# One block of a projection's products moved into the last softmax steps of the phase before it

## The reference

```python
proj = u @ w_in
qkv_a, z_a, b_a, a_a, q_b, k_b, v_b, gate_a, gate_b = jnp.split(proj, cuts, axis=-1)
qkv_a = silu(causal_depthwise_conv(qkv_a, conv_w))     # 3072 columns, for the delta rule
o_a = gated_delta_rule(q_a, k_a, v_a, g, beta)
y_b = window_attention(q_b, k_b, v_b, sinks, rel_bias) # softmax in bands of three chunks of 64
merged = sigmoid(gate_a) * y_a + sigmoid(gate_b) * y_b
```

## Time and profile before

| | us |
|---|---|
| median of 3 runs (1893.04 to 1895.02) | 1893.08 |
| the profiled execution | 1898.35 |
| its span, from first to last instruction | 1896.4 |
| TensorE busy in the span | 1743.6 |
| VectorE busy | 1428.1 |
| ScalarE busy | 1054.7 |

### The profile page before, as it was taken

One profiled execution on the slowest core, in us unless ns is written; L12 is line 12 of the kernel. 1 busy time (PEld: TensorE's weight loads), 2 busy tenths in 40 slices (PEclk: granted clock), 3 DMA queues, 4 the chain that ended last, 5 costly groups with the idle time before them and its releaser, 6 DMA issues. The chain is left out here.

```text
span 1896.4 us, 35111 instructions
## 1 busy us (share of the span) xinstructions
PE 1743.6 (92%) x14040; PEld 970.1 (51%) x14040; DVE 1428.1 (75%) x1786; ACT 1054.7 (56%) x1335; POOL 383.1 (20%) x262
## 2 busy tenths in 40 slices
PE   4999979999969999989999998499999999999965
PEld 1656654444448888734444455344554444444422
DVE  5556665878877889556766687799998888888928
ACT  3456653355444445342334211498898888888824
POOL 0000000110113434200000000234554344444300
PEclk9999999999988999999999998599999999999988
DMA  8500027563546232061223121599999999999935
GB/s 337 108 23 24 1 76 277 192 234 127 184 125 157 60 96 53 2 214 56 81 86 112 44 89 56 211 419 399 412 407 403 399 397 402 391 394 383 363 135 191
DMA packets 160441, 385.08 MB, mean 203 GB/s; under 512 B 24843, under 2 KB 102276, under 8 KB 132398
## 3 DMA queue, kind: packets, MB, share of 16 engines
q1 hardware_dynamic: 145710, 351.58, 51.0%
q0 software_dynamic: 14592, 31.56, 4.3%
HBM read 354.86 MB, written 48.15 MB: 213 GB/s over the span
## 5 line engine op out<-in xcount | busy, mean ns | idle before, releaser
L2298 PE MATMUL ps<-w_gate_up_split,gathered_t 128*128 128x512 f16 x1680 | 376.8, 381 | 7.7 <-ACT gathered_t L2372 3.3
L2464 DVE SCALAR_TENSOR_TENSOR w_gate_up_split<-w_staged,w_gate_up_split 128x2048 f16<-128x2048 f32 x140 | 318.3, 2288 | 55.0 <-ACT w_gate_up_split L2363 53.6
L2363 ACT ACTIVATE w_gate_up_split<-w_staged 128x2048 f16<-128x2048 f32 x140 | 266.5, 1908 | 44.2 <-DMA w_staged<-in_w_up 12.6
L2298 PEld LDWEIGHTS ps<-w_gate_up_split,gathered_t 128*128 128x128 f16 x1680 | 162.4, 98 | 203.5 <-ACT gathered_t L2372 10.4
L219 PE MATMUL ps<-u_transposed,w_gates_split 128*128 128x512 f16 x1152 | 254.3, 383 | 6.2 <-PEq L144 3.1
L825 PE MATMUL ps<-u_transposed,w_dense_split 128*128 128x512 f16 x1152 | 250.5, 379 | 0.8 <-PEq L450 0.8
L2325 PE MATMUL ps<-w_down_split,hidden_t 128*128 128x512 f16 x840 | 190.0, 383 | 7.6 <-ACT hidden_t L2409 5.2
L219 PEld LDWEIGHTS ps<-u_transposed,w_gates_split 128*128 128x128 f16 x1152 | 113.2, 99 | 146.8 <-issue 14.5
L825 PEld LDWEIGHTS ps<-u_transposed,w_dense_split 128*128 128x128 f16 x1152 | 112.0, 98 | 141.2 <-issue 6.9
L2464 DVE SCALAR_TENSOR_TENSOR w_down_split<-w_staged,w_down_split 128x2048 f16<-128x2048 f32 x70 | 159.4, 2287 | 20.6 <-ACT w_down_split L2363 20.5
L2363 ACT ACTIVATE w_down_split<-w_staged 128x2048 f16<-128x2048 f32 x70 | 133.3, 1907 | 45.4 <-DMA w_staged<-in_w_down 31.7
(11 more groups left out here) (359 smaller groups left out, 2894.4 us busy)
## 6 DMA issues: line engine op xcount, KB each, us to landing
w_staged<-in_w_gate SPq DMA_DIRECT2D x70, 1024.0 KB, 12.2
w_staged<-in_w_up SPq DMA_DIRECT2D x70, 1024.0 KB, 11.8
w_staged<-in_w_down SPq DMA_DIRECT2D x70, 1024.0 KB, 11.7
w_dense_ring<-in_w_in SPq DMA_DIRECT2D x17, 1024.0 KB, 7.5
w_ada_ring<-in_w_ada SPq DMA_DIRECT2D x8, 2048.0 KB
w_gates_ring<-in_w_in SPq DMA_DIRECT2D x24, 512.0 KB, 5.9
qkv_scratch<-delta_output POOLq DMA_DIRECT2D x20, 512.0 KB, 5.5
attention_output<-qkv_scratch SPq DMA_DIRECT2D x8, 1024.0 KB, 7.6
```

Of the source, the lines that this page charges most:

```text
L2298: last = pe.matmul(ps[:, GU[s] + j, :], xt[:, s, xp, k, :], w16[:, j, wp, k, :], start=(k == 0 and t == 0), stop=(k == KC - 1 and t == 2))
L2363: nc.scalar.activation(split(kind, 0, int(q)), staged(m, kind, int(q)), ACT.Identity, scale=W_SCALE).then_inc(hi_ok[kind + q], 1)
L2464: nc.vector.scalar_tensor_tensor(split(kind, 1, int(q)), staged(m, kind, int(q)), W_SCALE, split(kind, 0, int(q)), ALU.mult, ALU.subtract) ...
```

## The change

TensorE issues the 48 products of project's pair 0, block 0, in steps 24 to 32 of attention, behind `turn`, in nine portions of 5 or 6, into banks 2 and 3. The first of them waits for piece 5's split; the last raises the count that the query blocks raise. Project's pair 0 then sums block 1 alone. Block 0 is in banks 2 and 3 and block 1 in banks 0 and 1 from then on, and ScalarE's first copy waits for the raised count. The load of pair 2 (piece 7) goes to the end of attention's list of loads. Partial sums 0, 1 and 2 go behind the convolutions of their pairs, as sum 3 does.

```diff
@@ -446,6 +446,8 @@
     DENSE = 3 * TC
     PER_UNIT = 14
     ENDS = {(3 * KC * (j + 1) - 1) // PER_UNIT: j for j in range(4)}
+    NEXT = 5
+    FILL = 9
     SPLIT_AT = {first + q: (i, q) for i, first in ((3, 1), (4, TC), (5, 2 * TC), (6, 3 * TC)) for q in range(4)}
     with ExitStack() as ctx:
         w16 = m.w16
@@ -464,6 +466,7 @@
         k_ok, q_mm, q_ok, v_mm, v_used = (m.sem(n) for n in ("k_copied", "q_summed", "q_copied", "v_summed", "v_copied"))
         scores_mm, masked, max_ok, exps, p_ok, p_t, pt_ok, y_mm, y_ok = (m.sem(n) for n in (
             "scores_summed", "scores_masked", "max_ready", "exps_ready", "probs_ready", "probs_turned", "probs_turned_copied", "y_summed", "y_copied"))
+        m.q_mm = q_mm
         zeroed, dve_p = m.sem("attention_zeroed"), m.sem("dve_steps_attention")
         ps, sinks = m.ps, m.small[:, 16:32]
         place = lambda t: (t // TC, t % TC)
@@ -477,7 +480,7 @@
             for i in range(P // COPIES):
                 sp.dma_start(bias[i * COPIES:(i + 1) * COPIES], bass.AP(tensor=m.bias_dram.tensor, offset=127 - i * COPIES,
                              ap=[[QH * 320 - 1, COPIES], [320, QH], [1, KEYS]])).then_inc(bias_in, 16)
-            for i in range(2, 7):
+            for i in range(2, 8):
                 sp.wait_ge(m.w_lo, 4 * (i - 1))
                 load_dense(m, a, sp, i)
 
@@ -511,6 +514,17 @@
                         lo, hi = max(first, 3 * KC * j), min(end, 3 * KC * (j + 1))
                         if lo < hi:
                             q_unit(4 + 4 * qd + j, lo - 3 * KC * j, hi - 3 * KC * j)
+                elif part == 1 and t < DENSE + FILL:
+                    u = t - DENSE
+                    for n in range(6 * KC * u // FILL, 6 * KC * (u + 1) // FILL):
+                        half, n = n // (3 * KC), n % (3 * KC)
+                        if half == 0 and n == 0:
+                            pe.wait_ge(m.w_lo, 4 * (NEXT + 1))
+                        k, (wp, up) = n // 3, PASSES[n % 3]
+                        last = pe.matmul(ps[:, 2 + half, :], w16[:, NEXT % 2, wp, k, 0:P], m.u[:, up, k, half * 512:half * 512 + 512],
+                                         start=(n == 0), stop=(n == 3 * KC - 1))
+                    if u == FILL - 1:
+                        last.then_inc(q_mm, 1)
 
             def scores(t):
                 qd, c = place(t)
@@ -703,7 +717,7 @@
     KEYED = range(4, 8)
     LATE = 8
     ADA_AT = {0: (0,), 1: (1,), 2: (2,), 3: (3,), 8: (4, 5), 9: (6,), 10: (7,)}
-    PARTIAL_AT = {0: 0, 1: 1, 2: 2, 7: 4, 8: 5, 9: 6, 10: 7}
+    PARTIAL_AT = {7: 4, 8: 5, 9: 6, 10: 7}
     with ExitStack() as ctx:
         w16 = m.w16
         FIRST = 5
@@ -776,7 +790,8 @@
             sp.dma_start(m.yb_dram.rearrange("n p t -> p n t"), m.yb[:]).then_inc(yb_out, 16)
             load_ada(1)
             for p in range(2, PAIRS):
-                load(p)
+                if p > 2:
+                    load(p)
                 if p == 2:
                     sp.wait_ge(yb_out, 16)
                     load_z(0)
@@ -816,15 +831,15 @@
         def _(pe):
             def products(p):
                 pe.wait_ge(m.w_lo, 4 * (FIRST + p + 1))
-                for b in range(2):
+                for b in range(1 if p == 0 else 0, 2):
                     if p >= 1:
                         pe.wait_ge(copied, p * 2 + b - 1)
                     for half in range(2):
                         for n in range(3 * KC):
                             k, (i, j) = n // 3, PASSES[n % 3]
-                            last = pe.matmul(ps[:, 2 * b + half, :], w16[:, (FIRST + p) % 2, i, k, b * P:(b + 1) * P],
+                            last = pe.matmul(ps[:, 2 * (1 - b) + half, :], w16[:, (FIRST + p) % 2, i, k, b * P:(b + 1) * P],
                                              m.u[:, j, k, half * 512:half * 512 + 512], start=(n == 0), stop=(n == 3 * KC - 1))
-                    last.then_inc(mm, 1)
+                    last.then_inc(mm, 2 if p == 0 else 1)
 
             def extras(p):
                 if p in KEYED:
@@ -873,10 +888,13 @@
 
             def copy_out(p):
                 for b in range(2):
-                    act.wait_ge(mm, p * 2 + b + 1)
+                    if p == 0 and b == 0:
+                        act.wait_ge(m.q_mm, QH + 1)
+                    else:
+                        act.wait_ge(mm, p * 2 + b + 1)
                     if p >= 1:
                         act.wait_ge(conv_ok, p * 2 + b - 1)
-                    nc.scalar.activation(raw[:, b, 4:].rearrange("p (h t) -> p h t", h=2), ps[:, 2 * b:2 * b + 2, :],
+                    nc.scalar.activation(raw[:, b, 4:].rearrange("p (h t) -> p h t", h=2), ps[:, 2 * (1 - b):2 * (1 - b) + 2, :],
                                          ACT.Identity, scale=1.0 / W_SCALE).then_inc(copied, 1)
 
                     act.wait_ge(copied, p * 2 + b + 1)
@@ -1045,8 +1063,8 @@
                     residual(p - 2)
                 if p < PAIRS - 1:
                     convolve(p)
-                if p == 3:
-                    partial(3)
+                if p < 4:
+                    partial(p)
                 for n in ADA_AT.get(p - 1, ()):
                     row(n)
                 if p == 10:
```

## The result

The changed kernel took 1883.95 us (median of 6 runs, 1881.36 to 1887.94) beside 1894.13 for the kernel before, so the medians are 10.2 us apart. The ratio of the two is put at 0.9938, interval 0.9927 to 0.995, or 11.7 us less (9.5 to 13.8). Predicted were 1882.7, from a sum of 10.4. A second series of 5 runs gave 0.9959 (0.9946 to 0.9972), so 7.8 us (5.3 to 10.2). Both intervals take in 10, but the two series alone don't fix the gain to better than 5 to 14 us; the two stretches of the trace that the edits touch do. The profiled execution has a span of 1880.7 us.

The account below looks back on a forecast made before the run. TensorE bounds the projection; turn, ScalarE's copy and values pace the softmax tail. With 10.4 us removed from the projection and 0 added elsewhere, the median goes from 1893.08 to 1882.7 us, range 1878.5 to 1888.0.

Parts of the forecast that it names:

- Price of the block: Projection on TensorE: 48 products at 0.217 us each leave it, 10.4 us removed.
- Part 1: Softmax tail, steps 24 to 32: nine portions fit TensorE's 2.27 us holes behind the turn; 0 us added.
- the lower bound of -0.5: Softmax tail: least cost in us of all nine portions, 9 x -0.06, from step 22 with five products in place.
- Part 2: Projection without the block: everything TensorE's order drives comes 10.4 us earlier, with no late split; sums behind convolutions.
- The walk of VectorE: Projection: VectorE's new order stepped through with old durations; split margins of 7 us or more.
- The rival that VectorE gives the lead back: Projection: TensorE gains its lead but VectorE gives it back at the phase's end; 1893 us, chance 0.04.
- Part 3: Third pair's load issued early in the softmax phase: costs nothing there and covers a 3.5 us loss in the projection.
- Part 4: Bank swap, raised count and reordered semaphore waits: no added instruction, one wait already met; zero cost.
- Slower, by modulation loads in a loop: Projection: moved sums loop SP's modulation loads with the splits; 20.4 us lost against 10.4 won, 1903 us; chance 0.05.
- The clock falls elsewhere: Delta rule: clock falls land elsewhere relative to its work, some 4 us either way, 1878.7 or 1886.7; chance 0.12.
- The signs: Trace: holes about 2.27 us, project's first product about 272.5, delta rule's first inverse sum about 535.6, no split wait.

Follow-up runs that it names:

- before_turn: The changed kernel with each portion of products issued ahead of the step's turn instead of between turn and values; 0.9999 of the kernel before.
- five_holes: The changed kernel with the block's 48 products in five steps, 9 or 10 each, instead of nine; 0.9964 of the kernel before.
- old_sums: The changed kernel with partial sums 0, 1 and 2 back ahead of the convolutions, early load kept; 0.9977 of the kernel before.
- block_alone: The changed kernel with pair 2's load back inside project and partial sums 0, 1, 2 back ahead of the convolutions; 1.0017 of the kernel before.
- late_store: The changed kernel with pair 2's load back inside project and GpSimd's first two stores held until that load is split; 0.9948 of the kernel before.
- more: The changed kernel with six products in each of ten holes, 60 in all, project leaving out the extra 12; median 1881.64 us, 0.9926 of the kernel before.

## Why the prediction was right

- **Price of the block.** 10.4 us from 0.217 each; measured 264.77 - 254.42 = 10.35.
- **Part 1.** The holes take the portions. Taken as 0, measured 0.15. What failed in the small: a six was to come out at 2.17 us, below the hole, and came out at 2.32. The turn issued for 0.93 us in front of it (245.41 to 246.34) where I had read 0.87 in step 22, and six products take 1.39 up to the values where I had put 1.30. Step 22 was not a like case: its turn stands behind products, and behind products turn to values is 2.21 us with an empty hole too (`before_turn`), so the lower bound of -0.5 rested on a wrong reading. That `before_turn` loses all of it and `five_holes` some 4 us shows that the reason given, the loop of turn, copy and values, is the right one.
- **Part 2.** The walk of VectorE held within 0.4 us, and the splits kept their 7 us. Its reason for moving the sums, that they keep their loads' wait off the convolutions, is confirmed by `old_sums`: without it 7.4 of the 10.4 us are lost. The rival that VectorE gives the lead back does describe the kernels without the late sums (`old_sums`, and with the late load `block_alone`).
- **Part 3.** Nothing queued behind the early load, and it cost nothing, as said. The price of its cover was mis-sized: 3.5 us predicted, 8.7 measured. The step took the old landing time as fixed; but it moved, by the two stores that the block itself sends earlier (`late_store`: 2.97 us of wait without them, 6.00 with them), and a wait of TensorE had been priced at its length alone, without the products at half clock behind it (2.65 us). The number of DMAs ahead of the old load was misread too, seven issues on SP and not six, which changes nothing in the sum.
- **Part 4.** Zero: no wait appeared for banks or counts.
- **Slower, by modulation loads in a loop.** It did not come. Load 2 was issued at 318.73, earlier than the 321.2 of the walk, and sum 2 ran at 332.01 without waiting. What the rival named as its place (the sums' loads, with splits queued behind) is real, but in the old order of the sums.
- **The clock falls elsewhere.** The prediction gave it 0.12, as an effect of the change. What the record shows is a scatter that does not follow the change: the rest varies by 6 us among kernels with the same code there and does not go by the delta rule's start, and the changed kernel's own runs vary by 6.6 us. So the mechanism of the 10.4 us is shown by the stretches, but that the median of 1883.95 fell within 1.3 us of the forecast is in part luck: the second series had 1887.27. My argument against it, that three runs lay within 2 us, was too thin: 31 runs of the kernel before in one series spread from 1892.07 to 1899.44. The rule that was weighed there, of the Trainium skill's page TensorE: Matmul & The Clock Gate, Part 1 (the gate's looking does not start anew with the kernel), fits this scatter; no run here tests it by itself.
- **The signs.** Holes at 2.27: yes, 2.27 and 2.32. First product of project at 272.5: 272.88, of which 0.20 stood already ahead of step 24 (turn of step 23 at 232.98, before 232.78) and 0.15 the sixes. First inverse sum at 535.6: 536.21. No TensorE wait for a split: none.

## What to carry to other kernels

Work moved into another engine's latency is free only in the hole itself: find the instruction whose result the loop waits for, put the filler behind its issue, and size the portion by the hole (here five or six of 0.217 us in 2.27), since on the other side of that instruction the same filler costs its full length. When a bounding stage is shortened, walk every producer that feeds it, and the DMAs that the earlier results set off as well: here the two moves that were worth nothing alone kept 14.1 us of waits and slow products off, more than the block's gain. Price a stall of TensorE above its own length, because the products behind it may run at half clock.

## What the runs showed of the hardware

Stalls of TensorE of 6.00, 6.24, 3.50 and 3.60 us (the last with 1.24 idle shortly ahead of it) were each followed by products at the lower clock (0.50 to 0.58 granted in the first 2.5 to 4 us), 1.65 to 2.65 us of added time; the stall of 2.97 us was not. These are single profiles of each kernel. Two stores of 0.5 MB from GpSimd's queue, issued ahead, put off a 1 MB load of SyncE's queue by 3.0 us. And the end of the program, from the first product of the output projection to the last instruction, took 824 to 826 us in most of these profiles and 827.3 to 827.6 in four (the kernel before, the changed one again, `old_sums`, `more`), which no edit here explains.
